# Moving the weight ring of a two-layer trunk to another place in SBUF

## The reference

```python
mods = silu(c) @ w_ada + b_ada                      # shifts, scales and gates per sequence
h = rmsnorm(x) * (1 + sc1) + sh1
u = h @ w_in                                        # 1024 x 11264: two branches, gates
y_r = retention(...)                                # 8 heads, key 128, value 256
y_a = band_attention(...)                           # 8 heads of 128
mixed = sigmoid(m_r) * (y_r @ w_br_ret) + sigmoid(m_a) * (y_a @ w_br_att)
x = x + g1 * (mixed @ w_out)
h2 = rmsnorm(x) * (1 + sc2) + sh2
x = x + g2 * (relu(h2 @ w_up) ** 2 @ w_down)
```

## Time and profile before

| what | value |
| --- | --- |
| median of 3 runs | 1788.32 us (1788.06 to 1788.54) |
| profiled execution, its own time | 1787.66 us |
| its span, first to last instruction | 1786.1 us |
| TensorE busy | 1772.2 us, 99% |
| VectorE, ScalarE, GpSimd busy | 54%, 41%, 19% |
| granted TensorE clock | 1.00 |

### The profile page before, as it was taken

One profiled execution on the slowest core, in us unless ns is written; L12 is line 12 of the kernel. 1 busy time (PEld: TensorE's weight loads), 2 busy tenths in 40 slices (PEclk: granted clock), 3 DMA queues, 4 the chain that ended last, 5 costly groups with the idle time before them and its releaser, 6 DMA issues.

```text
span 1786.1 us, 34007 instructions
## 1 busy us (share of the span) xinstructions
PE 1772.2 (99%) x11773; PEld 1587.3 (89%) x11773; DVE 956.6 (54%) x1617; ACT 727.3 (41%) x1401; POOL 336.9 (19%) x454
## 2 busy tenths in 40 slices
PE   8999999999999999999999999999999999999999
PEld 6888888889999999999988888888899999999787
DVE  5456665657344575533364566666674346655343
ACT  3444444446322354432235444444453234554221
POOL 3433333330000210000022333333300003100100
PEclk9999999999999999999999999999999999999999
DMA  9566676665555623355536666666664535433842
GB/s 354 217 220 201 223 246 237 236 240 188 197 206 212 260 100 131 123 193 195 213 110 238 227 210 238 236 228 235 219 212 166 212 119 201 154 129 131 187 148 77
DMA packets 162736, 351.30 MB, mean 197 GB/s; under 512 B 78536, under 2 KB 90144, under 8 KB 154416
## 3 DMA queue, kind: packets, MB, share of 16 engines
q1 hardware_dynamic: 145584, 292.37, 47.6%
q0 software_dynamic: 9360, 47.62, 7.2%
q10 hardware_dynamic: 7664, 9.56, 1.5%
HBM read 314.86 MB, written 34.64 MB: 196 GB/s over the span
## 4 chain that ended last, share of the span: by engine, by line
PE 98%; DVE 1%; issue 0%; ACT 0%; DMA 0%; POOL 0%; DVEq 0%; SPq 0%
PE G L1658 43%; PE G L1694 32%; PE X L1821 8%; PE G L1969 5%; PE X L1969 3%; PE X L1717 2%; PE X L1626 2%; PE G L1938 2%; PE X L1694 1%; DVE wlo L1132 0%; DVE ysp L1446 0%; DMA xtok<-in_x_prompt_dram 0%; DVE hp L1195 0%; PE X L1711 0%; DVE rstd L1185 0%
## 5 line engine op out<-in xcount | busy, mean ns | idle before, releaser
L1132 DVE TENSOR_TENSOR wlo<-raw,whi 128x1024 fp32r<-128x1024 f32 x368 | 468.1, 1272 | 524.7 <-ACT whi L806 523.7
L806 ACT ACTIVATE whi<-raw 128x1024 fp32r<-128x1024 f32 x368 | 389.8, 1059 | 748.9 <-PE G L1658 347.0
L1694 PE MATMUL G<-whi,hhi 128*128 128x512 f32 x832 | 334.6, 402 | 1.2 <-DVE hlo L1200 0.9
L1694 PE MATMUL G<-wlo,hhi 128*128 128x512 f32 x832 | 324.9, 391 | 0.1
L1694 PE MATMUL G<-whi,hlo 128*128 128x512 f32 x832 | 324.4, 390 | 0.0
L1658 PE MATMUL G<-hhi,whi 128*128 128x384 f32 x704 | 236.8, 336 | 0.0
L1658 PE MATMUL G<-hhi,wlo 128*128 128x384 f32 x704 | 235.4, 334 | 0.0
L1658 PE MATMUL G<-hlo,whi 128*128 128x384 f32 x704 | 235.3, 334 | 0.0
L1694 PEld LDWEIGHTS G<-whi,hhi 128*128 128x128 f32 x832 | 156.2, 188 | 49.4 <-issue 13.4
L1658 PE MATMUL G<-ysp,whi 128*128 128x384 f32 x768 | 196.4, 337 | 0.0
L1694 PEld LDWEIGHTS G<-wlo,hhi 128*128 128x128 f32 x832 | 156.1, 188 | 34.5 <-DVE wlo L1132 0.6
(11 more groups left out here) (249 smaller groups left out, 2678.9 us busy)
## 6 DMA issues: line engine op xcount, KB each, us to landing
raw<-in_blocks_dram SPq DMA_DIRECT2D x368, 512.0 KB, 3.4
kc<-in_keys_dram SPq DMA_DIRECT2D x16, 1024.0 KB, 8.7
vc<-in_values_kept_dram SPq DMA_DIRECT2D x16, 1024.0 KB, 5.5
st<-in_states_dram POOLq DMA_DIRECT2D x16, 1024.0 KB, 7.1
out_dram<-st POOLq DMA_DIRECT2D x16, 1024.0 KB, 9.8
ada_w<-in_ada_dram SPq DMA_DIRECT2D x28, 512.0 KB, 5.4
ada_m<-in_ada_dram SPq DMA_DIRECT2D x20, 512.0 KB, 7.0
adaf_w<-in_ada_dram SPq DMA_DIRECT2D x10, 1024.0 KB, 7.6
```

The lines of the kernel that those rows point to most:

```text
L806: return a.activation(out, in_, ACT.Copy)
L1132: v.tensor_tensor(wlo[:, j % SPLIT, :, :], raw[:, j % RAW, :, :], whi[:, j % SPLIT, :, :].bitcast(F32), ALU.subtract).then_inc(blk_split, 1)
L1694: ins = t.matmul(B[banks[m][0]][:, :], x[:, kp * WK + k, m * P:(m + 1) * P], w[:, k, :], start=first and k == 0 and x is hhi and w is w_hi ...
```

## The change

Nothing that is computed, no instruction, no wait and no transfer is changed: only the places of buffers in SBUF. The calls that allocate `raw`, `whi` and `wlo` come last before the buffers of the stages, no longer first. `xT` comes behind `hlo`. `small` loses three columns that nothing reads, which moves nothing, since the next buffer begins at a multiple of 32 bytes all the same.

```diff
-    small = sb("small", [P, 64])
+    small = sb("small", [P, 61])
...
-    raw = sb("raw", [P, RAW, BK, BC])
-    whi = sb("whi", [P, SPLIT, BK, BC], F32R)
-    wlo = sb("wlo", [P, SPLIT, BK, BC], F32R)
-    xT = sb("xT", [P, KT, TOK])
     dstack = ExitStack()
...
     hhi = sb("hhi", [P, KT, TOK], F32R)
     hlo = sb("hlo", [P, KT, TOK], F32R)
+    xT = sb("xT", [P, KT, TOK])
...
     own_pair = sb("own_pair", [P, OWN])
+    raw = sb("raw", [P, RAW, BK, BC])
+    whi = sb("whi", [P, SPLIT, BK, BC], F32R)
+    wlo = sb("wlo", [P, SPLIT, BK, BC], F32R)
```

## The result

The kernel after takes 1795.18 us (median of 6 runs, 1794.92 to 1796.27), the kernel before 1788.3 us (6 runs): ratio 1.0041, 95% interval 1.0031 to 1.0051. It is slower by 6.9 us, on the side that was forecast, inside the range of 1782 to 1803 and inside the forecast's own range, 1792 to 1803. The profiled execution took 1794.92 us, its span is 1793.3 us.

The account below looks back on a forecast made before the run. The prediction took TensorE's row of matmuls, busy 99% of the span, as the bound. Terms 14.0 + 1.1 - 3.7 - 1.1 = +10.3 (or +9.9 by the other reading), taken as +10, gave 1798.3 us; range 1782 to 1803.

Parts of the forecast that it names:

- The bound and the covers: Whole kernel: matmul number times spacing sets the length; moved vector and scalar buffers and loads cost 0, rounds having room.
- The spacing depends on the remainders of the two operands: TensorE matmuls: places modulo 512 bytes, matched or not, set the spacing; 6.4 ns at 512 columns.
- L1694: Heads, 2592 matmuls 512 wide, matched before and unmatched after: 0 to +14.0 us, by width +14.0.
- L1969: Last stage, 576 matmuls 512 wide, unmatched before and matched after: 576 x 6.4 ns won, -3.7 us.
- The first rival: All matmuls: place costs nothing, L1969 is slow for its own reason; all terms 0, 1788.3 us, chance 0.26.
- the second: Ring's new place: distance or region counts and only helps; L1969 and slow turns gain, -4.8, 1783.5 us, chance 0.26.
- The reading by width: Newly unmatched streams: L1694 pays like 512 wide L1969, +14.0; 384 wide ones like out and down, +1.1 us.
- The reading by which operand is at 0: Newly unmatched streams: L1694 (moving at 0) pays 0; 384 wide ones (stationary at 0) pay like L1969, +14.7 us.
- The last rival: Every stream that loses its match pays the full 6.4 ns: +24, 1812 us, chance 0.10.
- Out and down: Out, down and merge's `ysp` part, 2304 matmuls, matched after: two slow turns of 192 matmuls end, -1.1 us.
- The 384 wide streams on `hhi`, `hlo`: L1658 and L1938, 2304 matmuls, unmatched after: slow turns at the rate of out and down, +1.1 us by width.
- the rule that spoke against it: Trainium skill on PE: separate operand ports, no waiting, no place cost beyond 16-byte lines; sum 0 instead of +10 us.

Follow-up runs that it names:

- e1: Kernel before with 32 bytes of padding ahead of the ring (`raw`, `whi`, `wlo`) and 480 behind, so remainder 0 in its old place: 1796.75 us, ratio 1.0044.
- e2: Kernel after with 480 bytes of padding ahead of the ring (`raw`, `whi`, `wlo`) and 32 behind, so remainder 480 in its new place: 1788.72 us, ratio 0.9996.
- m1: TensorE alone, trunk left out: rows of 36 matmuls at varied operand places; 512 columns take 226.7 ns matched, 233.3 ns with the stationary operand 64 ahead.
- e6: Kernel before padded so all places have remainder 0 modulo 512, except the ring (`raw`, `whi`, `wlo`) 256 bytes further: 1785.20 us, ratio 0.9982.
- the maps: m1 and a second such TensorE-only run with more offsets and the trunk's own reading orders; nothing below 226.7 ns at 512 columns or 173.3 at 384.

## Why the prediction was right

**The bound and the covers** held. TensorE's row of matmuls is the length; the rounding and the subtraction kept their durations (1059 and 1268 ns) and their waits (752.8 and 524.8 us), and the loads made ScalarE wait for 19.9 us where it had been 23.6. The term of 0 for them stands.

**The spacing depends on the remainders of the two operands: right, and shown by the runs.** It was an inference from one pair of streams, L1694 and L1969, that could have differed in something else. e1 and e2 separate remainder from distance, and m1 shows the 6.6 ns with everything else idle. The table of remainders modulo 512 was finer than it had to be: e6 and the maps show that 256 bytes apart is matched. The first rival (place is nothing) and the second (distance, gain alone) are refuted, the latter by e1 and e2 and by m1's rows with a buffer 152 KB further up. What in the engine or in the memory makes the difference stays open.

**Which reading: by width.** The forecast rested on a sum that two readings shared. The reading by width is the right one: all the loss is in the heads, 512 wide (L1694 from 226.9 to 233.1 ns), and none in the 384 wide streams on `hhi` and `hlo`. The reading by which operand is at 0 fails, since 512 columns are slow with either operand 32 off. The sums agreed by chance, and a reader should see that the number was luckier than its working. The last rival, both at once, has no part in it.

By the maps the nearest row for the 384 wide streams was picked on the wrong side, and luck covered it. After the change their stationary operand is at 0 and the moving one at 480, so the stationary one is 32 bytes ahead modulo 512. In the map, in L1658's order, that is (32, 0), 173.3 ns, and the streams stayed at that pace. Out and down before the change had it the other way, stationary at 480 and moving at 0: that is (0, 32), 176.7 ns, the pace of the two slow turns of the earlier trace rows. So by the map no slow turn was to be feared for `hhi` and `hlo`; a whole kernel with them 32 bytes ahead of the ring was not run. Why the other turns of out and down, and all of `ysp`, ran at the faster pace with the same remainders stays open; that the same two turns are slow in e2 speaks against chance.

**The terms.** L1969: -3.7 forecast, -4.1 measured. Out and down: -1.1 and -1.1. The 384 wide streams on `hhi`, `hlo`: +1.1 forecast, merge and up sum to +0.1. L1694: +14.0 forecast, +12.15 measured over the heads, the term that was furthest off. What was taken for lost already was about right: of the 2592 spacings behind an L1694 matmul, 2392 lie less than 14 ns over 226.7 in the trace of before, their mean is 227.9 ns, and 2.9 us are lost in them, where four openings of 0.04 us a turn made 2.6. What the term missed are the other 200: 93 lead to a matmul of another line and 107 last 300 ns and more, and neither kind is longer in the trace after. (2592 - 200) x 6.4 ns - 2.9 = 12.4 us, of which 12.15 were measured. Together +10.3 was forecast on the sum, +7.1 measured over the stages.

**On the rule that spoke against it.** Between rows that differ in place alone, 226.7 and 233.3 ns were measured with all other engines idle, in m1. The Trainium skill, page "SBUF — State Buffer", section "Who interferes with whom", gives the moving and the stationary operand a port each and has PE wait for nobody. L1694 has the same 226.7 ns between 925 and 965 us of the kernel before, with the other engines and the loads at work, so as far as other engines go the trace agrees; but the time of a matmul depends on where its two operands lie to each other, so they are not independent, and there the measurement decides.

## What to carry to other kernels

When TensorE's matmuls run back to back and reload their stationary operand each time, look at the distance between starts stream by stream: two streams of one shape with unlike spacings can differ by the places of their operands alone, as here. All of this was measured with fp32r operands and 128 stationary columns. In this kernel padding the buffers so that stationary and moving tiles start at equal remainders modulo 256 bytes took 0.2% off, and a move that broke this for the larger stream cost 0.4%; a stack of small buffers rounded up to 32 bytes breaks it without anyone asking. In this kernel what a new place is worth followed from which 512 wide stream had more matmuls (2592 in L1694, 576 in L1969), and so from reading addresses, not from how near the buffers lie.

## What the hardware showed that was not expected

- The shortest spacing in any place tried is 226.7 ns at 512 columns, 544 periods of the granted 2.4 GHz, and 173.3 ns at 384 columns, 416 periods. Both are 32 periods over the columns.
- Equal places are not best for all widths: 448 columns take 206.7 ns with both operands at 0 and 202.2 with the stationary one 64 off, 256 columns 120.0 and 113.3.
- It is not symmetric: at 512 columns the moving operand 64 bytes ahead costs 2.2 ns, the stationary one 64 ahead 6.6; at 384 columns in L1658's order the moving operand 32 bytes ahead costs 3.4 ns, the stationary one 32 ahead nothing.
- Both operands off by 4 bytes alike is the slowest row of all, 238.3 ns; equal remainders were fast at 32, 64, 96 and 480 bytes and slow at 4, 8, 16 and 24.
